# Wider map rings, a paced order of products, and two instead of three held query units in the gates-and-maps stage of a hybrid decoder step

## What is computed

```python
s = einsum('bqmhd,bkmhd->bmhqk', q, k) * DH_A ** -0.5      # m = 0, 1: the two maps
s = where(dist >= 0, s - slopes * dist, NEG_INF)
p = softmax(s); p = p[:, 0] - lam * p[:, 1]
o_a = einsum('bqk,bkd->bqd', p, v)
```

## Time and profile before

| what | value |
|---|---|
| median of 3 runs | 2535.59 us (2530.86 to 2535.63) |
| profiled execution, its own time | 2540.51 us |
| its span, first to last instruction | 2538.9 us |
| mean granted TensorE clock | 0.970 |
| PE busy | 2408.9 us, 95% of the span |
| DVE, ACT, POOL busy | 57%, 38%, 17% |
| `gates_and_maps` on PE | 949.2 to 1484.0 us, `attention_a` from 1494.8 us |

### The profile page before, as it was taken

The page is one execution under the profiler, slowest core; times in us unless marked ns, Lnnn a source line. Parts: engine busy times, 40 slices in busy tenths (PEclk is TensorE's granted clock), DMA queues, the critical chain, the costliest instruction groups (busy, mean ns, idle before and its releaser), DMA issues. The chain is left out here.

```text
span 2538.9 us, 34896 instructions
## 1 busy us (share of the span) xinstructions
PE 2408.9 (95%) x12466; PEld 1921.3 (76%) x12466; DVE 1436.6 (57%) x2444; ACT 957.2 (38%) x1605; POOL 434.6 (17%) x599
## 2 busy tenths in 40 slices
PE   5999999999999998989999979999999897999998
PEld 2788888887788876878787768877787754788886
DVE  3411335652666514757576756567878656665554
ACT  3211112224432222747575755444444433222221
POOL 0000112210222102545454541000000000000000
PEclk8999999999999999999999969999999998999999
DMA  8553545446454456676677469946466398544441
GB/s 293 216 219 147 196 152 163 157 153 236 132 161 125 148 210 173 223 220 197 218 234 233 154 211 340 290 89 131 96 135 159 108 327 276 178 141 145 145 142 54
DMA packets 329495, 465.19 MB, mean 183 GB/s; under 512 B 62513, under 2 KB 201665, under 8 KB 321326
## 3 DMA queue, kind: packets, MB, share of 16 engines
q1 hardware_dynamic: 322402, 434.35, 56.0%
q10 hardware_dynamic: 5888, 28.77, 2.9%
q0 software_dynamic: 1056, 0.13, 0.1%
HBM read 290.12 MB, written 173.04 MB: 182 GB/s over the span
## 5 line engine op out<-in xcount | busy, mean ns | idle before, releaser
L709 PE MATMUL proj_z<-first_km,h_hi 128*128 128x512 f32 x576 | 231.7, 402 | 3.2 <-DVE first_v L1273 3.2
L709 PE MATMUL proj_z<-first_km,h_lo 128*128 128x512 f32 x576 | 228.1, 396 | 0.0
L709 PE MATMUL proj_z<-first_v,h_hi 128*128 128x512 f32 x576 | 228.0, 396 | 0.0
L709 PE MATMUL proj_z<-proj_w_hi,h_hi 128*128 128x512 f32 x512 | 203.4, 397 | 0.0
L709 PE MATMUL proj_z<-proj_w_hi,h_lo 128*128 128x512 f32 x512 | 199.9, 391 | 0.0
L709 PE MATMUL proj_z<-proj_w_lo,h_hi 128*128 128x512 f32 x512 | 199.4, 389 | 0.0
L2057 POOL TENSOR_TENSOR map_plain<-map_plain,max_second 128x1024 f32<-128x1024 f32 (+4 forms) x96 | 166.8, 1747 | 146.4 <-ACT max_second L2170 146.4
L2567 ACT ACTIVATE map_plain<-att_b_s_ps 128x1024 f32<-128x1024 f32 (+2 forms) x160 | 142.3, 896 | 102.1 <-PE att_b_s_ps L2610 77.6
L2584 DVE TENSOR_TENSOR att_b_p_lo<-map_plain,map_region 128x1024 fp32r<-128x1024 f32 (+2 forms) x160 | 170.5, 1066 | 5.5
L1049 POOL TENSOR_TENSOR proj_rstd<-proj_rstd,keep_neg_half 128x8 f32<-128x8 f32 (+1 forms) x68 | 112.6, 1656 | 325.3 <-DVE proj_rstd L1371 325.3
L1239 ACT ACTIVATE proj_work<-proj_z 128x512 f32<-128x512 f32 x64 | 38.2, 597 | 273.0 <-PE proj_z L709 273.0
(11 more groups left out here) (446 smaller groups left out, 5939.3 us busy)
## 6 DMA issues: line engine op xcount, KB each, us to landing
w_raw<-in_w_in SPq DMA_DIRECT2D x144, 256.0 KB, 3.8
scratch_maps<-map_plain SPq DMA_DIRECT2D x40, 512.0 KB, 4.1
map_region<-scratch_maps SPq DMA_DIRECT2D x18, 1024.0 KB, 10.5
smp_v_a<-scratch_mixes SPq DMA_DIRECT2D x16, 1024.0 KB, 5.1
map_region<-scratch_q_hi SPq DMA_DIRECT2D x112, 128.0 KB
first_km<-scratch_w_split SPq DMA_DIRECT2D x20, 512.0 KB, 5.2
first_v<-scratch_w_split SPq DMA_DIRECT2D x20, 512.0 KB, 6.4
head_w<-in_w_ada SPq DMA_DIRECT2D x8, 1024.0 KB, 7.2
```

What stands on the lines that cost most here:

```text
L709: ins = nc.tensor.matmul(out, left(*lt), right(*rt), start=first and n == 0, stop=last and n == len(terms) - 1)
```

## The change

1. **Rings by width.** The first ring becomes 5120 columns (the old 4096 and a new tile `first` of 1024), the second 3072 as before, and a map takes only its own width in them. `ring_places` works out each map's place and which older maps lie there; the exponential waits for those (`first_over`, `second_over`). Map stores rotate over 8 semaphores in place of 4.
2. **Queries two deep.** Differential queries are held for two units and not three: a unit's load waits for the end of the unit two before. The 1024 columns of `map_region` set free take the "b" keys' first half, whose old place is the new tile `first`. The sum of SBUF stays the same.
3. **The planner.** It models the DMA traffic as one wire of 0.28 MB/us, in order, plus 2.2 us; products wait for their quarter's landing; the order of urgency on SP changes (`bq` and `follow` ahead of `map`); the loads at the start, of which all were issued ahead of the plan, are planned but for the first ones, and the first quarter of chunk 1 (`second`) is issued from 20 us on. Products get a quota in step with DVE's work, with 40 ahead and 16 kept to the end: past it a product is taken only when the next task is 1.2 us or more away.
4. **The end and the joint.** The last head ends with rows 1 and 0, and begins with 2 and 3. Two map blocks in place of six are loaded early, but already when the last head's upper rows have been scored. In `attention_a`, SP no longer waits for all map stores until block 6, and ACT and DVE wait for the gate stores before their first step, in place of SP.

What is computed, and the number of matmuls, reductions and exponentials, stay the same. The diff, cut to its core:

```diff
-              for part, count in ((a.region[:].bitcast(F32), 6), (a.plain[:], 2)) for i in range(count)]
+              for part, where in ((a.region[:].bitcast(F32), (0, 2, 1, 3, 4, 5)), (a.plain[:], (0, 1))) for i in where]
...
-MAP_PLACES, MAPS_EARLY = 8, 6
+MAP_PLACES, MAPS_EARLY = 8, 2
...
-LAST_ROWS = [*range(4), *range(TILES - 1, HALF - 1, -1), *range(4, HALF)]
+LAST_ROWS = [2, 3, *range(TILES - 1, HALF - 1, -1), *range(4, HALF), 1, 0]
 SEGS = HALF + 2 * HALF
-P0_RING, P1_RING = 4, 3
+STORE_SEMS, FIRST_COLS, SECOND_COLS = 8, 5 * 1024, 3 * 1024
...
+def ring_places(widths, columns):
+
+    at, live, places, over = 0, [], [], []
+    for i, w in enumerate(widths):
+        at = 0 if at + w > columns else 4 * 1024 if at < 4 * 1024 < at + w else at
+        over.append(sorted(y for lo, hi, y in live if lo < at + w and at < hi))
+        live = [(lo, hi, y) for lo, hi, y in live if y not in over[i]] + [(at, at + w, i)]
+        places.append(at)
+        at += w
+    return places, over
+
+
+RESERVE_FIRST, RESERVE_LAST = 40, 16
...
-    PRODUCT, COPY, ISSUE, LANDING, MARGIN, LATENCY = 0.229, 0.64, 0.62, 4.0, 0.1, 0.2
+    PRODUCT, COPY, ISSUE, LANDING, RATE, MARGIN, LATENCY = 0.233, 0.64, 0.57, 2.2, 0.28, 0.1, 0.2
...
+    quarter_in = {(0, q): 0.0 for q in range(4)}
+    wire = [10.0]
+    quota = [RESERVE_FIRST + (NP * EACH - RESERVE_FIRST - RESERVE_LAST) * sum(dve_us[:x]) / sum(dve_us) for x in range(N)] + [math.inf]
...
-    orders = [("bq", [(y, at_b[4 * (y - 2) + 3]) for y in range(2, len(at_b) // 4)]),
-              ("bk", [((i, half), at_b[24 * (i - 1) + (15, 23)[half]]) for i in range(1, HB) for half in range(2)]),
-              ("q", [((y, part), last_of(2 * (y - 3) + 1, 1)) for y in range(3, NG // 2) for part in range(4)]),
...
+    orders = [("bq", [(1, 0.0)] + [(y, at_b[4 * (y - 2) + 3]) for y in range(2, len(at_b) // 4)]),
+              ("bk", [((0, 1), 6.0)] + [((i, half), at_b[24 * (i - 1) + (15, 23)[half]]) for i in range(1, HB) for half in range(2)]),
+              ("q", [((1, part), 0.0) for part in range(4)]
+                 + [((y, part), last_of(2 * (y - 2) + 1, 1)) for y in range(2, NG // 2) for part in range(4)]),
...
-    urgent = ("map", "bq", "bk", "k", "q", "z", "follow", "rows", "early")
...
+    urgent = ("bq", "follow", "map", "bk", "q", "k", "z", "second", "rows", "early")
...
-            return task_end[N - 1] + LATENCY if queue_at["rows"] else never
+            return task_end[last_of(rows.index((HA - 1, HALF)), 1)] + LATENCY
+        if name == "second":
+            return 20.0
...
+            if m == 0 and j == 0:
+                other = max(other, quarter_in.get((c, quarter), never))
+            if q >= quota[x] and when - clock["pe"] < 1.2:
+                other = never
...
-            if m == 0 and seg >= P0_RING:
-                ready = max(ready, stored_end[seg - P0_RING] + LATENCY)
-            if m == 1 and seg >= P1_RING:
-                ready = max(ready, add_end[seg - P1_RING] + LATENCY)
+            if m == 0:
+                ready = max([ready] + [stored_end[y] + LATENCY for y in first_over[seg]])
+            if m == 1:
+                ready = max([ready] + [add_end[y] + LATENCY for y in second_over[seg]])
...
+            size = dict(z=0.26, follow=1.05, second=1.05, rows=0.13, early=1.3, bq=0.13, bk=0.27, q=0.10, k=0.20)
+            wire[0] = max(wire[0], clock["sp"] - ISSUE) + (0.512e-3 * wide_of[i] if what == "map" else size[what]) / RATE
+            landed = wire[0] + LANDING
...
-        q2, qm = region_part(k, 8 * 1024, 3, 2, 2 * P), region_part(k, 8 * 1024 + 12 * P, 3, 2, 2 * P)
-        second = sb("second", [P, P1_RING, 1024])
-        p0 = [a.plain[:, i * 1024:(i + 1) * 1024] for i in range(P0_RING)]
-        p1 = [second[:, i, :] for i in range(P1_RING)]
-        bk, bq = sb("bk", [P, 2, 1024], F32R), region_part(k, 11 * 1024, 2, 4 * P)
+        q2, qm = region_part(k, 8 * 1024, 2, 2, 2 * P), region_part(k, 9 * 1024, 2, 2, 2 * P)
+        second = sb("second", [P, SECOND_COLS])
+        more = sb("first", [P, 1024])
+        first_map = lambda seg, w: (more[:, first_places[seg] - 4 * 1024:first_places[seg] - 4 * 1024 + w] if first_places[seg] >= 4 * 1024
+                                    else a.plain[:, first_places[seg]:first_places[seg] + w])
+        second_map = lambda seg, w: second[:, second_places[seg]:second_places[seg] + w]
+        bk, bq = [region_part(k, 10 * 1024, 1024), sb("bk", [P, 1024], F32R)], region_part(k, 11 * 1024, 2, 4 * P)
...
-                    if m == 0 and seg >= P0_RING:
-                        act.wait_ge(k.map_stored[seg % P0_RING], 16 * (seg // P0_RING))
-                    if m == 1 and seg >= P1_RING:
-                        act.wait_ge(comb_done, seg - P1_RING + 1)
-                    dst = (p1[seg % P1_RING] if m else p0[seg % P0_RING])[:, 0:width[x]]
+                    if m == 0:
+                        for y in first_over[seg]:
+                            act.wait_ge(k.map_stored[y % STORE_SEMS], 16 * (y // STORE_SEMS + 1))
+                    if m == 1 and second_over[seg]:
+                        act.wait_ge(comb_done, second_over[seg][-1] + 1)
...
                     if what == "q":
                         y, part = i
-                        sp.wait_ge(s_done, last_of(2 * (y - 3) + 1, 1) + 1)
+                        if y >= 2:
+                            sp.wait_ge(s_done, last_of(2 * (y - 2) + 1, 1) + 1)
...
                     if what == "early":
-                        sp.wait_ge(s_done, N)
-                        sp.wait_ge(k.shift_stored, 32)
+                        sp.wait_ge(s_done, last_of(rows.index((HA - 1, HALF)), 1) + 1)
...
-                maps_stored(k, sp, HA)
-                for done, count in k.max_out_stored:
-                    sp.wait_ge(done, count)
                 out_of = 0
                 sp.wait_ge(k.shift_stored, 32)
                 for b, (h, g, kg) in enumerate(blocks):
+                    if b == 6:
+                        maps_stored(k, sp, HA)
...
+                gates_stored(k, act)
+                gates_stored(k, dve)
```

More of the change, by code:

```diff
@@ L1674, with gates_stored, joint_plan @@
 MAP_ROWS = list(range(HALF)) + list(range(TILES - 1, HALF - 1, -1))
-LAST_ROWS = [*range(4), *range(TILES - 1, HALF - 1, -1), *range(4, HALF)]
+LAST_ROWS = [2, 3, *range(TILES - 1, HALF - 1, -1), *range(4, HALF), 1, 0]
 SEGS = HALF + 2 * HALF
-P0_RING, P1_RING = 4, 3
+STORE_SEMS, FIRST_COLS, SECOND_COLS = 8, 5 * 1024, 3 * 1024
+def gates_stored(k, eng):
+    for done, count in k.max_out_stored:
+        eng.wait_ge(done, count)
 def maps_stored(k, sp, heads):
     for slot, done in enumerate(k.map_stored):
-        sp.wait_ge(done, 16 * len(range(slot, heads * SEGS, P0_RING)))
-def joint_plan(tasks, rows, width, last_of, at_b, rank_b, at_map, segments, pieces, ends, released, TURN, R, BANKS):
+        sp.wait_ge(done, 16 * len(range(slot, heads * SEGS, STORE_SEMS)))
+def ring_places(widths, columns):
[8 more added lines that the diff above has]
+RESERVE_FIRST, RESERVE_LAST = 40, 16
+def joint_plan(tasks, rows, width, last_of, at_b, rank_b, at_map, segments, pieces, ends, released, TURN, R, BANKS, first_over, second_over):
     never = math.inf
@@ L1873, in joint_plan @@
             queue_at[what] += 1
+            clock["sp"] = start + dict(bk=2, follow=2, second=2, rows=2, early=8).get(what, 1) * ISSUE
+            size = dict(z=0.26, follow=1.05, second=1.05, rows=0.13, early=1.3, bq=0.13, bk=0.27, q=0.10, k=0.20)
+            wire[0] = max(wire[0], clock["sp"] - ISSUE) + (0.512e-3 * wide_of[i] if what == "map" else size[what]) / RATE
+            landed = wire[0] + LANDING
             if what in ("map", "z"):
[L1875 to L1880, removed]
+                (stored_end if what == "map" else z_stored)[i] = landed
+            if what == "second":
+                quarter_in[1, 0] = landed
+            if what == "follow":
+                c, quarter = i // 4, i % 4
+                quarter_in[(c + 1, quarter + 1) if quarter < 3 else (c + 2, 0)] = landed
+            if what in ("map", "z", "follow", "second", "rows", "early"):
                 made.sp.append((what, i))
@@ L1950, in gates_and_maps @@
     R, BANKS = 3, 6
-    plan = joint_plan(tasks, rows, width, last_of, at_b, rank_b, at_map, segments, pieces, ends, released, TURN, R, BANKS)
+    first_places, first_over = ring_places([wide(rows[g][1], kh) for g, kh in segments], FIRST_COLS)
+    second_places, second_over = ring_places([wide(rows[g][1], kh) for g, kh in segments], SECOND_COLS)
+    first_over = [sorted({*over, *([s - STORE_SEMS] if s >= STORE_SEMS else [])}) for s, over in enumerate(first_over)]
+    plan = joint_plan(tasks, rows, width, last_of, at_b, rank_b, at_map, segments, pieces, ends, released, TURN, R, BANKS, first_over, second_over)
     place, held = plan.place, plan.held
@@ L2264, in score_b @@
                         w = min(512, width[x] - c0)
```

(2 more changed lines are left out.)

74 lines of the change are left out of this document (39 added, 35 removed).

## The result

The changed kernel takes 2490.07 us (median of 4 runs, 2488.92 to 2491.03) against 2535.58 for the kernel before (2530.86 to 2535.63): 45.5 us less, a ratio of 0.9825 with a 95% interval of 0.9808 to 0.9842. The forecast was 2498.6 in a range of 2472 to 2526.

The account below looks back on a forecast made before the run. PE was taken as the bound, its stage losing 80.2 us. Tail 25, joint -3, between 13, start 5 and queries -3 sum to 37 us saved, giving a median of 2498.6 us, range 2472 to 2526.

Parts of the forecast that it names:

- Tail: End of the changed stage, where only scores are left: loss falls from 31.0 to 6 us, 25 saved (12 to 27).
- Joint: Passage into `attention_a`: a late third map block may stall PE; 3 us lost, bounds 0 and 7.
- Start: Stage's first 50.8 us: loads no longer ahead of early "b" queries save 5 of 18.4 us lost, bounds 0 and 10.
- Between and queries: Stage between start and tail: rings save 13 of 30.8 us (0 to 26); two query units lose 3 (0 to 15).
- 0.3 to 1.8 us to spare: Query loads: a unit's load of 5.9 to 7.4 us fits the shortest unit, 7.7 us, if SP is free.
- Tail only: Rival, chance 0.18: waits between stay or move to other loads; gain about 16 us, time 2513 to 2531.
- Slower, the body opens: Rival, chance 0.09: held-back products leave gaps, the whole stage runs at the tail's low clock; 18 us more, 2554.
- All of it: Rival, chance 0.09: the new plan leaves hardly an idle slot; gain 59 us, time 2465 to 2483.
- The products, the clock at the end and ACT's waits: Signs: products run to within some 10 us of the last score, clock near 1.00, `scratch_maps` waits under 15 us.
- the last gap: Sign at the stage's end: PE's last gap before L2444, the next stage, is 5 to 8 us.
- The three holes: Windows at 1110 to 1133, 1190 to 1223 and 1360 to 1390 us, 24.3 us lost in sum, shrink to half.
- the sign of too shallow a query ring: Sign at a head's first rows: PE waits for `scratch_q` would show the two-unit query ring as too shallow.

## Why the prediction was right, and where it was off

The forecast was 37 us of gain, the result 45.5, by the mechanisms that it named. Of its terms three were too low and one too high, so the sum is nearer than some of its parts.

- **Tail**, 25 against 27.3 us measured. Right in size and cause: without the quota 19 us are lost, and the tail is back at half clock. In the reason for the shorter drain it was wrong. It came from narrow last rows in the prediction; the old order drains as quickly. The kept products run on PE meanwhile, and SP's queue is free of the 15 early loads, which the prediction did not count as part of the drain.
- **Joint**, 3 lost in the forecast. Nothing was lost: `attention_a` took 172.4 us against 175.7, and PE had no wait for map blocks or values in it. The third block was issued at 1443.42 and used at 1449.66 without a wait, so it had landed in 6.2 us at most. The bound of 0 was the right one. The estimate of 4.4 us by the Trainium skill ("DMA: Bandwidth & Descriptors", Anatomy of one DMA — SWDGE) agrees with this; the median of 10.5 us, taken from blocks with others queued ahead, does not.
- **Start**, 5 against 12.1. The term was too small: it counted PE's named waits, and took it that the half clock of the first products would stay. In the changed kernel's profile the stage began at full clock, some 2.4 us of luck. 6 us come of the order of the loads, and the rest is not settled.
- **Between and queries**, 13 - 3 = 10 against 6.3. ACT's waits for stores fell from 39.0 to 0.7 us, and the rings by themselves are worth 19 in the whole kernel; two units cost about 7 and not 3. The "0.3 to 1.8 us to spare" for a unit's load had no ground: the landings of 3.5 and 5.0 us in it are those of six other DMAs. By the semaphores' events a unit's load took 7.4 us in the median and up to 11.8 already in the kernel before, against the 7.7 us of the shortest unit, so there was nothing to spare at a change of head.
- **Rivals.** "Tail only" fell: the old rings cost 19 us. "Slower, the body opens" fell too. In the changed kernel two stretches of 100 us run gapless at full clock with quotas on. "All of it" was not reached by the changed kernel; the version with queries and keys first, at 2481.9, came to the edge of its range.
- **Signs.** The products, the clock at the end and ACT's waits came as the prediction said, and the last gap, 4.8 us, just below its 5 to 8. The three holes did not shrink to half: they lose 18.7 us and not 24.3, and lie at the changes of head, two of them at a DMA share of 1.05 and 1.08. PE's waits for queries at a head's first rows, the sign of too shallow a query ring, came too.

What remains open: part of the start's gain, the worth of the planner's wire, and how much of each difference of 6 to 8 us is the luck of a plan.

## What to carry to other kernels

Count the instructions of the bounding engine in a stretch without gaps and at full clock, and price each stage by that pace; the rest is the loss, and it can be placed. Where filler work hides the gaps of a chain, ration it over the whole chain, for what is left at the end runs uncovered and at the low clock; a rationed filler also covers the drain. When a buffer is cut so that another can grow, measure both sides alone: here 1024 columns were worth about the same in either place. When small changes to a planner are compared, measure first how far two plans of the same rules lie apart, with more than one of them. And see that a landing time in a view of a tile belongs to the DMA in question: here the median of 3.5 us was that of another stage's stores.

## What the runs showed of the hardware

In the tail of the kernel without the quota PE was busy for 24.7 of 30.7 us and still had a granted clock of 0.55, while windows of the changed kernel with 8.6 of 10 us busy kept 1.00. After the same gap of 3.6 us the stage began at half clock in one profile (that of the kernel before, 0.76 over the first 10.8 us) and at full clock in the thirteen others; what decides this the runs don't show. The last of a unit's four query loads landed 2.3 to 13.5 us after its issue in the changed kernel, by its semaphore's events, and the longest times fell where the DMA share was 1.05 (1094.5 to 1118 us). Another order of the same work, from a planner's cost changed by 1%, moved the median by 2.4 us, the ratio to the kernel before by 0.003, and the stage of a single profile by 5 us.
